# First modulation of a two-block transformer kernel cut by quarters of the features instead of by halves

## What is computed

```
shift, scale, gate = split(silu(c) @ w_mod[l] + b_mod[l], 3)     # also for the context, with c_ctx
h  = rms_norm(x, g_pre[l]) * (1 + scale) + shift
z  = h @ w_in[l]                                                 # split into 11 branches of 512 and the gates
log_gamma = -softplus(-ret_decay_logit[l])                       # decay rates of the retention branch
```

## Time and profile before

| | us |
|---|---|
| median of 3 runs without a profile | 1771.73 (1771.65 to 1771.84) |
| the profiled execution, its whole time | 1771.81 |
| span of that execution, first to last instruction | 1769.9 |
| PE busy | 1751.0 |
| first matmul of any kind | 7.62 |
| first matmul of RK | 22.46 |
| first matmul of DQ | 63.10 |

### The profile page before, as it was taken

The page is one execution under the profiler, slowest core; times in us unless marked ns, Lnnn a source line. Parts: engine busy times, 40 slices in busy tenths (PEclk is TensorE's granted clock), DMA queues, the critical chain, the costliest instruction groups (busy, mean ns, idle before and its releaser), DMA issues.

```text
span 1769.9 us, 25341 instructions
## 1 busy us (share of the span) xinstructions
PE 1751.0 (99%) x8975; PEld 1462.3 (83%) x8975; DVE 915.6 (52%) x1855; ACT 1021.1 (58%) x1503; POOL 1365.6 (77%) x573
## 2 busy tenths in 40 slices
PE   7999999999999999999999999999999999999998
PEld 4888888888888888888888878898888887888887
DVE  2885544977745447675338973321113985332112
ACT  4645676445677654466565667455555576745554
POOL 5867788976778878677879756888887965679886
PEclk9999999999999999999999999999999999999999
DMA  9875656754566667455657544556665654456663
GB/s 367 311 249 156 189 169 215 235 167 143 160 195 193 178 207 245 134 163 160 199 143 217 176 131 131 180 177 190 190 190 174 203 155 131 135 187 192 190 188 130
DMA packets 172051, 329.47 MB, mean 186 GB/s; under 512 B 10512, under 2 KB 16176, under 8 KB 171952
## 3 DMA queue, kind: packets, MB, share of 16 engines
q1 hardware_dynamic: 168336, 320.24, 58.4%
q10 hardware_dynamic: 3616, 7.90, 1.3%
HBM read 327.03 MB, written 1.06 MB: 185 GB/s over the span
## 4 chain that ended last, share of the span: by engine, by line
PE 69%; POOL 14%; issue 14%; DMA 1%; POOLq 0%; ACT 0%; DVE 0%; SPq 0%; DVEq 0%; ACTq 0%
PE G L1968 16%; PE G L1970 16%; PE G L1969 16%; POOL wlo L537 14%; PE A L2657 3%; PE G L2657 3%; PE A L1968 2%; PE A L1970 2%; PE A L1969 2%; PE A L2658 1%; PE G L2658 1%; PE A L2433 1%; PE G L2448 1%; DMA raw<-in_w_in 1%; PE A L2022 1%
## 5 line engine op out<-in xcount | busy, mean ns | idle before, releaser
L537 POOL TENSOR_TENSOR wlo<-raw,whi 128x1024 fp32r<-128x1024 f32 (+1 forms) x568 | 1361.9, 2409 | 390.7 <-ACT whi L562 387.2
L562 ACT ACTIVATE whi<-raw 128x1024 fp32r<-128x1024 f32 (+1 forms) x568 | 593.5, 1048 | 567.3 <-PE G L1970 436.6
L1968 PE MATMUL G<-whi,hparts 128*128 128x512 f32 (+1 forms) x1472 | 578.3, 393 | 1.0 <-DVE hparts L1300 0.6
L1970 PE MATMUL G<-whi,hparts 128*128 128x512 f32 (+1 forms) x1472 | 567.7, 386 | 0.0
L1969 PE MATMUL G<-wlo,hparts 128*128 128x512 f32 (+1 forms) x1472 | 567.4, 385 | 0.0
L1968 PEld LDWEIGHTS G<-whi,hparts 128*128 128x128 f32 x1472 | 276.4, 188 | 60.0 <-issue 5.9
L1970 PEld LDWEIGHTS G<-whi,hparts 128*128 128x128 f32 x1472 | 276.3, 188 | 56.2
L1969 PEld LDWEIGHTS G<-wlo,hparts 128*128 128x128 f32 x1472 | 276.7, 188 | 52.0
L1893 DVE TENSOR_TENSOR G<-G,frelu 128x512 f32<-128x512 f32 x12 | 8.4, 700 | 188.9 <-ACT frelu L1134 188.9
L1719 DVE STREAM_TRANSPOSE t<-z 32x256 f32<-32x256 f32 (+2 forms) x256 | 96.8, 378 | 3.8
L1968 PE MATMUL G<-whi,osplit 128*128 128x512 f32 x240 | 94.2, 393 | 0.0
(11 more groups left out here) (430 smaller groups left out, 2514.6 us busy)
## 6 DMA issues: line engine op xcount, KB each, us to landing
raw<-in_w_in SPq DMA_DIRECT2D x324, 512.0 KB, 3.7
raw<-in_w_up SPq DMA_DIRECT2D x64, 512.0 KB, 3.7
raw<-in_w_down SPq DMA_DIRECT2D x64, 512.0 KB, 3.3
raw<-in_w_out SPq DMA_DIRECT2D x40, 512.0 KB, 3.7
raw<-in_w_branch_out SPq DMA_DIRECT2D x36, 512.0 KB, 4.4
modw<-in_w_mod SPq DMA_DIRECT2D x32, 512.0 KB, 5.4
raw<-in_w_branch SPq DMA_DIRECT2D x24, 512.0 KB, 3.2
modz<-in_w_mod SPq DMA_DIRECT2D x16, 512.0 KB, 10.0
```

The costliest lines, as they stand in the source:

```text
L537: pool.tensor_tensor(wlo[:, s, :, 0:n], raw[:, s, :, 0:n], whi[:, s, :, 0:n].bitcast(F32), ALU.subtract)\
L562: act.activation(whi[:, slot, :, 0:n], raw[:, slot, :, 0:n], ACT.Copy).then_inc(hi_ready, 1)
L1968: pe.matmul(bank, hi, whi[:, slot, kk, 0:n], start=first, stop=False)
L1970: return pe.matmul(bank, lo, whi[:, slot, kk, 0:n], start=False, stop=last)
```

## The change

The first modulation is made by quarters of the features. A modulation slab is now 512 rows by 256 columns, the same 512 KB, in runs of 1 KB where they were of 2 KB. A quarter needs four slabs (shift and scale, each in two halves of the rows), so PE, ACT and DVE go through rows, copy, turn and shift-and-scale four times instead of twice. The weight slabs go in the order of k: RK, RQ and DKc of quarter 0, then of quarter 1, and so on. Ahead of the first weight slab stand four modulation slabs; the other twelve, three turns and the tokens of quarters 2 and 3 are put between the weight slabs. Decay rates and two memsets move behind quarter 0 in DVE's stream, and their exponential on ACT moves behind the second `split`. ACT's wait for a copy of RK, RQ or DKc now has slab 13, 14 or 15 behind each (before: slab 11, 13 and 15, with 10, 12 and 14 ahead). The 28 unread transposes stay, in another bank.

```diff
-        HB_FIRST = [A[0], A[1], A[3], A[2]]
+        HB_FIRST = [A[0], A[3], A[3], A[3]]
...
-        MOD_FIRST = {(1, 1): 3, (2, 0): 1, (2, 1): 4, (0, 3): 1, (1, 3): 1, (2, 3): 1}
+        QUARTERS = [(c, s) for s in range(SLOTS) for c in range(3)]
+        MOD_FIRST = {(1, 0): 2, (2, 0): 2, (0, 1): 2, (1, 1): 2, (0, 2): 2, (1, 2): 2, (0, 3): 1, (1, 3): 1, (2, 3): 1}
... (SP)
+                    h, part = divmod(q, 2)
+                    src = flat["w_mod"][part * D // 2:(part + 1) * D // 2, h * D + c * MODN:h * D + (c + 1) * MODN]
...
-            for _ in range(2 * SLOTS):
+            for _ in range(SLOTS):
                 mod_slab()
... (ACT)
                 mod_copy()
                 split(0)
+                quarter(0)
+                split(1)
+                act.wait_ge(lg_ready, w(lg_ready))
+                act.activation(lgt[:, 2], lgt[:, 1], ACT.Exp, scale=-1.0).then_inc(lg_exp, 1)
+                split(2)
+                mod_copy()
                 split(3)
+                quarter(1)
+                for n in (4, 5, 6):
+                    next_split(n)
+                mod_copy()
+                quarter(2)
                 act.dma_start(const[:, N_FIRST:], g["p_const"][:, N_FIRST:]).then_inc(consts_in, 16)
                 tables(0)
+                for n in (7, 8, 9):
+                    next_split(n)
+                mod_copy()
+                quarter(3)
+                for n in (10, 11, 12):
+                    next_split(n)
                 for c, col in enumerate((RK, RQ, DKc)):
-                    act.wait_ge(weights_used, w(weights_used))
-                    split((2 * c + 2) % SLOTS)
                     for t in range(TT):
                         act.wait_ge(projected, w(projected))
                         act.activation(z[:, t, col:col + W], ...).then_inc(evacuated, 1)
-                    split((2 * c + 3) % SLOTS)
+                    split((13 + c) % SLOTS)
... (DVE)
+                    for q in range(SLOTS):
+                        first_shift_scale(q)
+                        stream_low(0, (q,))
+                        if q == 0:
+                            decay_rates()
... (PE)
+                next_mods(SLOTS)
+                turn_tokens(normed, HB_FIRST, (0,))
+                next_turn(0)
+                turn_tokens(normed, HB_FIRST, (1,))
+                for r in range(28):
+                    pe.transpose(A[1][:, r % 4 * P:(r % 4 + 1) * P], normed[:, 0, r % 8 * P:(r % 8 + 1) * P], ident)
+                for n, (c, s) in enumerate(QUARTERS):
                     pe.wait_ge(lo_ready, w(lo_ready))
+                    if c == 0:
                         pe.wait_ge(h_split, w(h_split))
+                    part(n, c, s, 0)
+                    if c == 1 and s == 0:
+                        next_mods(2)
+                    if c == 1 and 0 < s < SLOTS - 1:
+                        next_turn(s + 1)
+                    part(n, c, s, 1)
+                    if c == 0 and s == 0:
+                        next_mods(2)
+                    if c == 1 and s == 0:
+                        next_turn(1)
+                    if c == 0 and 0 < s < SLOTS - 1:
+                        turn_tokens(normed, HB_FIRST, (s + 1,))
+                        next_mods(SLOTS)
```

More of the change, by code:

```diff
@@ L1234, in mod_slab @@
                     for a, bank, kept in mod_accs(c):
-                        row = cond[:, 8 + 32 * k + a:9 + 32 * k + a]
+                        row = cond[:, 16 + 32 * k + a:17 + 32 * k + a]
                         if k == 0:
@@ L2155, in mod_slab @@
                 mods["n"] += 1
-                c, q = MOD_ORDER[i // SLOTS], i % SLOTS
+                c, q = divmod(i, SLOTS)
                 pe.wait_ge(modz_full[i % MODZ], w(modz_full[i % MODZ], 16))
[L2158 to L2163, removed]
+                h, part = divmod(q, 2)
+                for kk in range(KT // 2):
+                    ins = pe.matmul(bank[32 * kk:32 * kk + 32, 0:MODN], cond[:, 16 + 32 * (part * KT // 2 + kk) - 8 * h - 2 * c:][:, 0:32],
+                                    modz[:, i % MODZ, kk], start=q == 0,
+                                    stop=q == SLOTS - 1, skip_group_check=True)
                 ins.then_inc(mod_used, 1)
             def mod_turn(bank, src):
-                turned_rows = bank[:, MODN:MODN + 4 * KT].rearrange("p (c j a) -> p j c a", j=2, a=2)
+                turned_rows = bank[:, MODN:MODN + 4 * KT].rearrange("p (h q j a) -> p j q h a", h=2, j=2, a=2)
                 for j in range(2):
@@ L2173, in first_chunks, with part @@
             def first_chunks():
-                def part(n, c, s, fresh=False):
+                def part(n, c, s, t):
+                    bank = (G[0:2], G[2:4], A[0:2])[c][t]
+                    for kk in range(SLAB_K):
+                        k = s * SLAB_K + kk
+                        cols = slice(t * P, (t + 1) * P)
+                        ins = product(bank[:], hhi[:, k, cols], hlo[:, k, cols], n % SLOTS, kk, CH, k == 0, k == KT - 1)
+                    if s == SLOTS - 1:
+                        ins.then_inc(projected, 1)
+                    elif t == TT - 1:
+                        ins.then_inc(weights_used, 1)
@@ new lines, in next_mods, with next_turn @@
+                def next_mods(count):
+                    for _ in range(count):
+                        mod_slab(A[2])
+                def next_turn(s):
+                    if s > 0:
+                        pe.wait_ge(modT_ready, w(modT_ready))
+                    pe.wait_ge(mod_copied, w(mod_copied))
+                    mod_turn(A[2], modrow)
+                pe.wait_ge(silu_c, w(silu_c))
+                next_mods(SLOTS)
+                pe.wait_ge(ident_in, w(ident_in, 16))
+                pe.wait_ge(norm_ready, w(norm_ready, TT))
@@ L2176, in part @@
+                turn_tokens(normed, HB_FIRST, (0,))
[3 more added lines that the diff above has]
+                    pe.transpose(A[1][:, r % 4 * P:(r % 4 + 1) * P], normed[:, 0, r % 8 * P:(r % 8 + 1) * P], ident)
+                for n, (c, s) in enumerate(QUARTERS):
                     pe.wait_ge(lo_ready, w(lo_ready))
-                    if fresh:
+                    if c == 0:
                         pe.wait_ge(h_split, w(h_split))
-                    banks = (G[0:2], G[2:4], A[0:2])[c]
@@ L2212, in first_chunks @@
-                for n, (c, s) in enumerate(HALVES[1]):
-                    part(n + len(HALVES[0]), c, s, c == 0)
+                    part(n, c, s, 0)
[8 more added lines that the diff above has]
+                        next_turn(1)
```

97 lines of the change are left out of this document (22 added, 75 removed).

## The result

The changed kernel takes 1775.88 us (median of 14 runs, 1774.33 to 1776.23) against 1771.82 (14 runs, 1771.65 to 1772.10): ratio 1.002, 95% interval 1.0013 to 1.0027. It is slower by 4.1 us, 0.23%, and lies above the stated range. The profiled execution took 1775.87, its span is 1773.9.

What follows compares the result with a forecast made beforehand. PE was taken to bound the kernel behind the head, so DQ's shift passes to the end: -3.66 at the start, +2.2 on PE, +1.7 at DQ, +0.2 us in sum, giving 1771.9; range 1769.4 to 1774.5.

Steps and rivals of the forecast that it cites:

- From turn to first projection before took ... 4.14 us: Head, quarter 0: turn to first projection takes 4.14 us as before, so its data is ready at 17.9 to 18.0.
- the lower bound of 18.4: Start of first projection: earliest time, with the 28 unread transposes at the higher level; 18.8 taken, upper bound 20.75.
- The wait at quarter 1, "+0.9": First slab of quarter 1: turn to `h_split` takes 4.14, PE has only 0.47 + 2.72; wait 0.9, bounds nothing and 0.95.
- The second rival: Head: the lower clock lasts, first projection at 20.75, all behind it 1.95 later, 1773.9 us; chance 0.16.
- The wait at DQ, 1.7: End of head: ACT's copies stand behind slab 13's split; PE, ready at 61.6, waits 1.7 until 63.3; bounds 61.6 and 65.0.
- Runs of 1 KB, 0.05 us a slab: Modulation slabs' DMA: shorter runs cost 0.05 us a slab, 0.2 for four; bounds nothing and 0.19 a slab.
- Costed at nothing: Head: moved decay rates (4.2 us), their exponential's table load and split 7 (POOL done near 46, wanted 47.4) delay nothing.
- 63.3: Start of DQ on PE as forecast, 0.2 us later than before.

Runs made afterwards that it cites:

- the last pair: Changed kernel with scale in PSUM, turn 1 earlier, 12 unread transposes, rates behind quarter 1, tables behind quarter 3: 1770.67 us with slab 13 first, 1771.93 with SP's order unchanged.

## Why the prediction was wrong, step by step

**The step that failed: "From turn to first projection before took ... 4.14 us".** It took 20.23 - 14.18 = 6.05. The link was right in its instructions and wrong in their durations: it took DVE's multiply from the one place in the trace of before where POOL stood idle (POOL began at 19.65; the multiply had taken 0.17 us at 19.25). But before, the multiply was short by a margin of 0.4 us only. The kernel before, ACT, then DVE:

```profile
18.51 1.06 ACT L562 ACTIVATE whi<-raw 128x1024 fp32r<-128x1024 f32 x1 [0.24 <-DMA raw<-in_w_in]
```

```profile
19.25 0.17 DVE L1277 SCALAR_TENSOR_TENSOR modT<-modT,small 128x8 f32<-128x8 f32 x1
...
41.11 1.31 DVE L1277 SCALAR_TENSOR_TENSOR modT<-modT,small 128x8 f32<-128x8 f32 x1
```

The changed kernel, ACT:

```profile
13.41 0.38 ACT L747 ACTIVATE modrow<-A 128x256 f32<-128x256 f32 x1 [3.70 <-PE A L2164]
13.69 1.05 ACT L561 ACTIVATE whi<-raw 128x1024 fp32r<-128x1024 f32 x1
```

Counted from the start of ACT's copy of the rows, POOL's subtract comes earlier than it did and the multiply later. The split that the subtract follows starts 0.28 us behind that start instead of 0.63, as it no longer waits for its slab; the turn starts 0.77 behind it (14.18 - 13.41) instead of 0.44 (18.32 - 17.88), as four transposes at the lower level stand ahead of it. So the multiply, which came 0.40 us ahead of the subtract, now comes 0.23 behind it (15.05 against 14.82). The other multiply of before, at 41.11, had taken 1.31 us beside a subtract, with no wait of PE behind it; the row was there and was not read. The Trainium skill, "GPSIMD Engine Reference", section "8. Key points", says that GpSimd shares its SBUF interfaces with VectorE and contends with VectorE instructions in a 2-port performance mode or with two SBUF inputs; for the multiply the traces agree (0.16 us with an operand in PSUM, 1.65 to 2.14 with both in SBUF). The Trainium skill, "Trainium Architecture — The Big Picture", section "What this means for kernel authors", calls the sharing an exclusive lock; the multiply ends at 17.19 and the subtract at 17.18, which fits.

PE's own part was right: with the transposes at the higher level it would have been ready at 18.3, near the lower bound of 18.4. The start was missed by 1.43 us.

**The wait at quarter 1, "+0.9".** Its mechanism was right, its size not: from turn to first matmul 35.34 - 29.84 = 5.50, not 4.14, by the same hold, so 2.11 (+1.2).

**The clock.** The second rival had the lower level last beyond the unread transposes, and in the changed kernel they ran at the higher level (3.22 us). It fell afterwards instead, behind the idle 1.90 us, for 1.7 us of loss. The rival's price, half of each us at the lower level, held; its place did not. In profiles of other versions the 28 transposes began at the lower level and took 3.39 to 4.57 us, so there the rival came true in part. The Trainium skill's rule in "TensorE: Matmul & The Clock Gate", section "Part 4: PE-mode transpose", is that the full clock does not engage for transposes. The traces do not agree with it for these transposes: 28 of them kept the higher level here, at 0.115 us each, and with the scale formed in PSUM the level rose within them, from four ahead of them in 1.09 us at 14.90 to 28 in 3.82 us that ended at the higher level. What raised it stays open.

**The wait at DQ, 1.7.** Right by its chain: the split of slab 13 waits for its slab (3.70 on ACT), which SP issued at 60.34 behind a modulation slab. It measured 0.98 instead of 1.7. Both ends of the wait hang on turn 3 (53.21), so that PE was late did not shorten it: the chain behind the turn took 67.09 - 53.21 = 13.88 instead of 14.4, mainly as its first link, up to the end of the split, took 3.80 instead of 4.14, and PE's own path took 12.9 instead of 12.7.

**Runs of 1 KB, 0.05 us a slab.** The four slabs came 1.41, 1.51 and 1.50 us apart, where the kernel before had 1.43, 1.36 and 1.35: 0.28 us over the three gaps, 0.09 a slab and 0.15 for the later two, inside the bounds and above the value taken. The DMA view reads 361 GB/s, with weight slabs in runs of 2 KB among them, against 386 for 2 KB alone. Behind the first four PE waited for no modulation slab.

**Costed at nothing.** Right for split 7 and for the exponential. For the decay rates it was right only while the start is late: they were through at 27.6, ahead of turn 1 at 29.84; in the version with 12 unread they held up quarter 1 by 2.19.

The sum, from 63.3 to 67.09: +1.43 at the start, +1.7 of the clock, +1.2 at quarter 1, -0.7 at DQ, and +0.2 that is left unnamed. The hold is behind the first and the third: with it removed at both places 2.4 us came back. For the clock's term only the order of events is shown, the idle time and then the fall.

In six profiles a fall came within about 1 us behind a wait of 1.9 to 2.1 us: in the changed kernel and with turn 1 earlier at the start (1.94, 1.97), with POOL's subtract later, with 45 transposes and with the decay rates ahead at quarter 1 (2.11, 2.12, 2.12), and with 12 unread and the rates behind quarter 1 at turn 3 (1.92). No fall came behind waits as long in the changed kernel's own quarter 1 (2.11), with slab 13 first (2.12), with 12 unread (2.19), and with 28 unread and the rates behind quarter 1 (2.04). So idle time of that length is not enough by itself, and what decides stays open. So does why the changed kernel's 14 runs lie in two groups (six at 1774.3 to 1775.0, eight at 1775.9 to 1776.2), of which one has been seen in a profile; a low stretch in the one and not in the other would come near their distance, but that is not shown.

What the change was worth without the holds is seen in the last pair: with the multiply, the turn, the unread transposes (12 for 28), the rates, the tables and SP's order mended, DQ starts 2.5 us earlier than before in the first one's profile. 1.6 us of that reach the end of the span (1768.3 against 1769.9): two waits behind DQ that the kernel before does not have, one for DVE (0.39 us at 63.88) and one for POOL (0.21 at 932.95), take 0.6 of the rest. The median is 1.1 us below that of before, within noise.

## What to carry to other kernels

When a step moves, ask what runs on the other engines at its new time, and take each duration from a row in which they do. In the rows read here, a small VectorE instruction with its inputs in SBUF, in the chain to PE's start, cost as much as what was left of the GpSimd subtract beside it, and an add or a multiply with one input in PSUM did not. A head in which four engines hand on in turn gives little for one edit: each mended wait here uncovered the next one (transposes, decay rates, a transfer), and only all of them together came below the time of before, by 1.1 us, which is within noise. Idle time of PE costs more than itself where the lower clock follows it.

## What was not expected of the hardware

- VectorE instructions of 0.16 to 0.2 us took up to 2.27 us beside a GpSimd subtract of 2.36 to 2.4 us, until it ended: a multiply with two inputs in SBUF (2.14), but also a copy (1.67, 2.27) and a TENSOR_SCALAR (2.21) with one. With an operand in PSUM the multiply took 0.16. A row of 16 TENSOR_SCALAR steps took 7.51 us beside two subtracts and 9.49 beside three.
- TensorE went to half its granted clock not in an idle stretch of 1.9 us but up to 1 us after it, with matmuls running back to back, and stayed there for about 3.4 us. This followed six waits of 1.9 to 2.1 us and did not follow four of 2.0 to 2.2 us.
- The same 28 transposes took 3.22, 3.82 and 4.41 us in three versions whose start differed by under 1 us (15.07, 15.79, 15.98).
